# Where the weight splits and GpSimd's share run in the later stages of a two-block transformer kernel

## The chip, the cores and the metric

The program runs on one core of one Trainium2 chip. The metric is the device time of one execution in microseconds; the comparison is by the median over runs.

## The reference

The input is 256 tokens of width 1024, all in float32. The first block is a mixer, a cross attention over 256 memory rows, and a mixture of 32 experts (the best four for each token). The second block has two layers:

```python
for layer in range(2):
    h = x * (1.0 + scale) + shift
    y = mixer_ab(h, ...) if layer % 2 == 0 else mixer_c(h, ...)
    x = layer_norm(DN_ALPHA * x + gate * y, ln_g[layer, 0], ln_b[layer, 0])
    h = x * (1.0 + scale) + shift
    y = jnp.square(jax.nn.relu(h @ mlp_w1)) @ mlp_w2
    x = layer_norm(DN_ALPHA * x + gate * y, ln_g[layer, 1], ln_b[layer, 1])
```

`mixer_ab` projects h (1024 to 1224 columns), applies rope, and runs a windowed attention with sinks (8 heads) and one over the 64 best keys of an index score (8 heads). `mixer_c` has 16 heads with plain causal attention at this length. Both end in an output projection of 1024 by 1024. The MLPs go from 1024 to 4096 and back.

## The kernel before, in words

Five engines run their own programs and meet at semaphores. The file has one section for each: `block.sync` (SP, which issues the loads), `block.gpsimd`, `block.scalar` (ScalarE, ACT), `block.tensor` (TensorE, PE) and `block.vector` (VectorE, DVE).

**Weights as granules.** All weights go through a ring of 8 slots of 128 x 4096 float32 (2 MB each). One load is a granule, numbered in the order in which TensorE uses them. TensorE adds one to `granules_used` (`used`) when it has finished with one. The expert loop takes slots 0 to 5 (`E_SLOTS` is 4, 5, 2, 3, 0, 1), six granules for each of 32 experts: four of the gate and up projection, two of the down projection. The granules after the experts are, in order, ab_in (3), uq (1), ab_out (2), mlp0 (16), c_in (6), c_out (2), mlp1 (16). They land in `POST_SLOTS`, four slots in turn: 6, 7, 4, 5.

**Splits.** A product outside the experts is made in three passes over two reduced-precision parts of each operand: high by high, high by low, low by high (`three`, L1047). So each granule after the experts but uq is split before use. `split_hi` (L477, always on ScalarE) copies it to its high part; `split_lo` (L487, on VectorE or GpSimd) subtracts the high part from the raw weights to get the low part. `split_no` numbers the splits; the semaphores `w_hi` and `w_lo` count them, and each waits for the one before it. The kernel before has two pairs of high and low slots (`PAIRS`: slots 2, 3 and 0, 1), used in turn. A split can begin when TensorE is done with the split two before. A raw slot can be loaded again when both its parts are made.

**Who does what around the splits.** Each engine's order is written out by hand; a wait holds everything behind it on that engine. GpSimd makes the low parts of the first granule of each stage (ab_in 0, ab_out 0 and 1, mlp0 0, c_in 0, c_out 0 and 1, mlp1 0). It multiplies the normalised X by the norm's gain and adds its bias (`affine`, L649), for the final norm of the first block and for three layer norms; the transposed copy that feeds the matmuls has gain and bias folded in elsewhere, so this X is needed only for the next residual sum. It also ropes the window attention's queries (L424 to L427). VectorE does the other low parts, the other ropes, the masks and softmax pieces, the layer norms (`layer_norm`, L1989 to L1999), the low part of the transposed activations (`evac_lo`, L2016 and L2021), and the low part of the MLP's hidden values (L2033, L2037). ScalarE does the high parts, PSUM evacuations, exponentials and roots.

**Order at the joints.** After a layer norm, TensorE transposes X (L1412), ScalarE and VectorE write the high and low transposed chunks, and the next matmuls begin chunk by chunk (`x_chunk`). In an MLP, groups of four granules (w1, w2, w1, w2) repeat four times; ScalarE and VectorE split the granules two ahead after each pair of hidden halves. After the expert loop TensorE scatters the last expert's output (L1288), VectorE adds the sums to X (L1884) and scales it by the final norm's root (L1888). If an expert had more than 64 tokens, extra passes follow the loop, up to 16, read from a table.

The pairs and the raw slots are laid out in these lines:

```python
SLOTS = 8
R2 = 4
POST_SLOTS = [6, 7] + E_SLOTS[0:2]
PAIRS = (E_SLOTS[2:4], E_SLOTS[4:6])
```

Of the kernel before, what the change touches and what calls it, by code (L numbers as in the profile page):

```python
# [22 lines left out]
ALU = mybir.AluOpType  # L23
# [6 lines left out]
TB = S // P  # L30
D = 1024
KC = D // P
NE = 32
# [95 lines left out]
PAIRS = (E_SLOTS[2:4], E_SLOTS[4:6])  # L129
# [79 lines left out]
def build_program(nc, A, tab_d, dft_d, out_d):  # L209
    ctx = ExitStack()  # L210
    with ctx:
# [16 lines left out]
        def sb(name, shape, dt=F32):  # L228
# [8 lines left out]
                  for part, s in zip(("hi", "lo"), slots)] for i, slots in enumerate(PAIRS)]  # L237
# [53 lines left out]
        def pair(n):  # L291

            return [part[:] for part in pairs[(n - 1) % 2]]
# [171 lines left out]
        def split_hi(act, name, i, it=None):  # L465

            g = granule_no(name, i)
            n = split_no(g)
# [8 lines left out]
            act.activation(pair(n)[0][:, 0:w], slot(slot_of(g), w), ACT.Copy).then_inc(sem("w_hi"), 1)  # L477

        def split_lo(eng, name, i, it=None):
# [3 lines left out]
            hi, lo = pair(n)  # L483
# [8 lines left out]
        def _(sp):  # L492
# [67 lines left out]

            sp.wait_ge(sem("table_ready"), 1)
            n = nc.values_load(table_i[0:1, 32:33], engines=[ENG.SP], min_val=0, max_val=NX_MAX)
            with sp.If(n > 0):
                sp.wait_ge(used, MOE_END)
                with sp.Fori(0, n) as i:
                    e = nc.values_load(table_i[0:1, bass.ds(i, 1)], engines=[ENG.SP], min_val=0, max_val=NE - 1)
                    sp.wait_ge(sem("extra_used"), i + 1)
                    for j in range(PER_E):
                        sp.dma_start(slot(expert_slot(j)).rearrange("p (k n) -> p k n", k=2 if j < 4 else 4),
                                     expert_source(j, e)).then_inc(sem("extra_landed"), 16)  # L570
# [3 lines left out]
            for name, count in (("ab_in", 3), ("uq", 1), ("ab_out", 2), ("mlp0", 16), ("c_in", 6), ("c_out", 2),  # L574
                                ("mlp1", 16)):
                if name[:3] != "mlp":
                    for i in range(count):
                        o = OWNER[g]
                        if o is None:
                            sp.wait_ge(used, NPRE)  # L580
                        elif o < MOE_END:
                            sp.wait_ge(used, o + 1)
                        else:
                            sp.wait_ge(sem("w_hi"), split_no(o))
                            sp.wait_ge(sem("w_lo"), split_no(o))
                        for dst, src in granule_source(name, i, slot_of(g)):
                            sp.dma_start(dst, src).then_inc(landed[slot_of(g)], 16)
                        g += 1
                    continue
                if name == "mlp0":  # L590
                    sp.wait_ge(*done("uq", 0))
# [3 lines left out]
                with sp.Fori(0, 4) as i:  # L595
                    for j in range(R2):
                        s = slot_of(g + j)
                        n = split_no(g + j) - R2
                        sp.wait_ge(sem("w_hi"), i * R2 + n)
                        sp.wait_ge(sem("w_lo"), i * R2 + n)  # L600
# [15 lines left out]
        def _(pool):  # L616
# [24 lines left out]

            def w_lo(name, i):
                split_lo(pool, name, i)

# [1544 lines left out]
```

## Time and profile before

| | us |
|---|---|
| median of 3 runs | 2086.86 |
| all runs | 2105.39, 2086.86, 2086.72 |
| the profiled execution, whole | 2106.02 |
| its span, from first to last instruction | 2104.2 |
| busy in the span: TensorE | 1881.5 (89%) |
| VectorE | 751.7 (36%) |
| ScalarE | 538.4 (26%) |
| GpSimd | 140.7 (7%) |

The span is one profiled execution; the positions in the rows (1379.67, for example) are microseconds from its start. Busy time counts an instruction from its start to its end, whatever it waits for inside. The expert loop lies between about 350 and 1320 us, the stages that the change touches from there to the end. Line numbers such as L487 are lines of the kernel before; where a helper issues an operation, the line is the helper's. PEclk is the TensorE clock that was granted, 1.00 for full speed.

### The profile page before, as it was taken

What the parts mean: (1) busy time and instruction counts of PE and PEld (TensorE: products, weight loads), DVE (VectorE), ACT (ScalarE), POOL (GpSimd) and SP (SyncE); (2) the same over time, 40 slices, a digit from 0 to 9 for tenths busy, and PEclk for the clock granted to TensorE, in tenths of its full rate; (3) what the DMA queues carried; (4) which work ended last, traced back from release to release, by engine and by line L of the source; (5) the groups of instructions that cost most, each with busy time, mean ns of one, the idle gap of its engine ahead of it and who ended that gap; (6) DMA issues with size and microseconds to landing.
All of it is one profiled execution on the core that took longest, in us unless ns stands there. A gap on an engine that the chain in (4) does not pass through costs nothing.

```text
span 2104.2 us, 25272 instructions
## 1 busy us (share of the span) xinstructions
PE 1881.5 (89%) x10270; PEld 1155.1 (55%) x10270; DVE 751.7 (36%) x1136; ACT 538.4 (26%) x700; POOL 140.7 (7%) x49
## 2 busy tenths in 40 slices
PE   6998898999999999999999999755699979568997
PEld 6855665434444344433443344634589868357996
DVE  3323232111111111111111111477565476656555
ACT  4322341111111111111111111335334432533442
POOL 0100110000000000000000000240300030311000
PEclk9998895999999999999999999866799989888999
DMA  8488568899999999999999999440145535213450
GB/s 310 166 303 331 177 227 334 356 417 417 419 418 417 417 419 418 417 417 419 418 417 417 419 418 416 156 159 1 60 154 185 200 120 192 88 60 117 164 179 21
DMA packets 136599, 587.07 MB, mean 279 GB/s; under 512 B 6446, under 2 KB 6660, under 8 KB 102756
## 3 DMA queue, kind: packets, MB, share of 16 engines
q1 hardware_dynamic: 135108, 581.25, 70.0%
q10 hardware_dynamic: 1440, 5.11, 0.7%
q8 instruction: 36, 0.59, 0.1%
q14 instruction: 15, 0.12, 0.0%
HBM read 585.29 MB, written 1.05 MB: 279 GB/s over the span
## 4 chain that ended last, share of the span: by engine, by line
PE 62%; DMA 20%; DVE 13%; ACT 3%; issue 2%; SPq 0%; POOL 0%; ACTq 0%; DVEq 0%
PE bank L1047 29%; DMA ring<-in_w_gate_up 20%; PE bank L1255 14%; PE bank L1279 5%; PE bank L1215 3%; PE bank L1118 2%; PE bank L1288 1%; DVE sb_X L1992 1%; PE bank L1108 1%; DVE arena_r L2021 1%; DVE sb_XN L1962 1%; PE bank L1246 1%; PE bank L1381 1%; PE bank L1272 1%; DVE sb_XN L1933 1%
## 5 line engine op out<-in xcount | busy, mean ns | idle before, releaser
L1255 PE MATMUL bank<-ring,arena 128*64 128x512 f32 x2048 | 458.6, 598 | 8.0 <-DMA ring<-in_w_gate_up 8.0
L1255 PEld LDWEIGHTS bank<-ring,arena 128*64 128x64 f32 x2048 | 140.3, 137 | 321.0 <-issue 298.5
L1047 PE MATMUL bank<-w_hi,arena_r 128*128 128x512 f32 (+1 forms) x784 | 259.5, 393 | 6.5 <-DVE arena_r L2037 3.7
L1279 PE MATMUL bank<-ring,arena 128*64 128x512 f32 x1024 | 226.8, 595 | 0.0
L487 DVE TENSOR_TENSOR w_lo<-ring,w_hi 128x4096 fp32r<-128x4096 f32 (+2 forms) x37 | 161.6, 4367 | 134.0 <-ACT w_hi L477 133.8
L477 ACT ACTIVATE w_hi<-ring 128x4096 fp32r<-128x4096 f32 (+2 forms) x45 | 160.6, 3577 | 131.3 <-PE bank L1047 130.7
L1047 PEld LDWEIGHTS bank<-w_hi,arena_r 128*128 128x128 f32 x784 | 149.3, 190 | 37.2 <-DVE arena_r L2037 4.1
L487 POOL TENSOR_TENSOR w_lo<-ring,w_hi 128x4096 fp32r<-128x4096 f32 (+1 forms) x8 | 70.6, 8821 | 1366.2 <-ACT w_hi L477 1365.8
L825 ACT ACTIVATE arena<-arena,sb_tab 128x512 f32<-128x512 f32 x32 | 23.1, 722 | 530.0 <-DVE arena L1826 530.0
L1047 PE MATMUL bank<-XT_r,w_hi 128*128 128x256 f32 x512 | 147.8, 289 | 12.0 <-DVE arena_r L2021 12.0
L1800 DVE TENSOR_SCALAR arena<-sb_tab,sb_pos 128x64 f32<-128x64 f32 x66 | 13.8, 252 | 400.0 <-PE bank L1255 400.0
L1279 PEld LDWEIGHTS bank<-ring,arena 128*64 128x64 f32 x1024 | 70.7, 137 | 153.9 <-issue 153.9
L1826 DVE TENSOR_SCALAR arena<-bank 128x512 f32<-128x512 f32 x32 | 22.1, 692 | 351.5 <-PE bank L1255 351.5
L1047 PE MATMUL bank<-arena_r,w_hi 128*128 128x256 f32 x512 | 146.5, 286 | 0.0
L1047 PE MATMUL bank<-XT_r,w_lo 128*128 128x256 f32 x512 | 146.4, 286 | 0.0
L1215 PEld LDWEIGHTS bank<-arena,sb_XN 128*128 128x128 f32 x1056 | 123.7, 196 | 26.0 <-issue 26.0
L1215 PE MATMUL bank<-arena,sb_XN 128*128 128x64 f32 x1056 | 128.2, 281 | 0.0
L1047 PE MATMUL bank<-w_lo,arena_r 128*128 128x512 f32 x320 | 125.6, 392 | 0.0
L1047 PEld LDWEIGHTS bank<-XT_r,w_hi 128*128 128x128 f32 x512 | 99.7, 195 | 14.6 <-issue 14.1
L1047 PEld LDWEIGHTS bank<-arena_r,w_hi 128*128 128x128 f32 x512 | 99.9, 195 | 0.9 <-issue 0.5
L1047 PEld LDWEIGHTS bank<-XT_r,w_lo 128*128 128x128 f32 x512 | 99.9, 195 | 0.0
L462 DVE TENSOR_TENSOR half_lo<-ring,half_hi 128x2048 fp32r<-128x2048 f32 x22 | 50.4, 2292 | 85.0 <-ACT half_hi L452 84.8
(318 smaller groups left out, 2376.3 us busy)
## 6 DMA issues: line engine op xcount, KB each, us to landing
ring<-in_w_gate_up SPq DMA_DIRECT2D x128, 2048.0 KB, 23.1
ring<-in_w_down SPq DMA_DIRECT2D x64, 2048.0 KB, 22.3
ring<-in_mlp_w SPq DMA_DIRECT2D x32, 2048.0 KB, 8.2
ring<-in_ada_w SPq DMA_DIRECT2D x24, 2048.0 KB, 9.4
ring<-in_c_w_in SPq DMA_DIRECT2D x6, 2048.0 KB, 7.6
ring<-in_w_in SPq DMA_DIRECT2D x4, 2048.0 KB, 7.6
ring<-in_w_k SPq DMA_DIRECT2D x2, 2048.0 KB, 12.2
ring<-in_w_v SPq DMA_DIRECT2D x2, 2048.0 KB, 21.2
```

The lines of the kernel that those rows point to most:

```text
L462: eng.tensor_tensor(lo[:], half_raw(name, h)[1], hi[:].bitcast(F32), ALU.subtract).then_inc(sem("w_lo"), 1)
L477: act.activation(pair(n)[0][:, 0:w], slot(slot_of(g), w), ACT.Copy).then_inc(sem("w_hi"), 1)
L487: eng.tensor_tensor(lo[:, 0:w], slot(slot_of(granule_no(name, i)), w), hi[:, 0:w].bitcast(F32), ALU.subtract).then_inc(sem("w_lo"), 1)
L825: act.activation(sig, gcl, ACT.Sigmoid, bias=zero, scale=1.702).then_inc(sem("e_sig"), 1)
L1047: mm = pe.matmul(out, st[a], mv[b], start=start and a + b == 0, stop=stop and a == 1, skip_group_check=True)
L1108: mm = pe.matmul(B[7][:, c:c + 1], part[:, c * P:(c + 1) * P], quads[:, 0:1], start=True, stop=True)
L1118: mm = pe.matmul(B[6][32 * c:32 * c + 32, :], cs[:, 2 * c + r, :], w[:, 2 * c + r, :], start=(r == 0), stop=(r == 1))
L1215: mm = pe.matmul(B[3][:, k * CAP:(k + 1) * CAP], XN[:, t, k * P:(k + 1) * P], sel_tok[:, t, :], start=(t == 0), stop=(t == 1))
L1246: pe.matmul(B[m][CAP * h:CAP * h + CAP, :], selG[64 * m:64 * m + NE, :], rows[:, h * HW:(h + 1) * HW], start=True, stop=False)
L1255: mm = pe.matmul(B[m][CAP * h:CAP * h + CAP, :], xe[:, 2 * j + kl, :], w[:, kl, m * D + h * HW:m * D + (h + 1) * HW], start=False, stop=(j ...
L1279: mm = pe.matmul(B[2][CAP * h:CAP * h + CAP, :], hT[:, c, CAP * j:CAP * j + CAP], w[:, c, h * HW:(h + 1) * HW], start=False, stop=(j == 1 ...
L1826: dve.tensor_scalar(gcl, B[0][:], 7.0, None, ALU.min).then_inc(sem("e_clamp"), 1)
```

## The change

Only the work after the expert loop is touched, in six ways.

1. Slots: four granules can be split at once. The high part of a granule has one of four slots of its own (`HI_SLOTS`: 2, 3, 0, 1) and its low part is written over the raw weights. A slot is loaded again when TensorE has used the granule in it.
2. GpSimd does no low parts, no `affine` and no rope after the expert loop. VectorE does them, at other places of its order.
3. ScalarE's high parts move: ab_in 0 in the last expert (which is peeled off the loop), ab_in 1 where ab_in 0 was, c_out 0 and 1 before the values of the second attention are evacuated, mlp 0 and 1 before the gate rows, c_in 0 inside the last MLP group.
4. VectorE's order: ab_in 0 after the expert loop, ahead of the residual additions; ab_in 1 before the rope angles; ab_out 0 before the first scores; ab_out 1 and mlp0 0 and 1 before the first layer norm; the first MLP group is peeled so that the affine of the norm before stands behind it; c_in 0 in the last MLP group; c_out 0 and 1 before the second attention; mlp1 0 and 1 before the third norm.
5. SP issues ab_in 0 and 1 before it looks at the table of extra experts.
6. The extra passes use slots 4, 5, 0, 1 (`X_SLOTS`), and load the down granules after the gate and up products.

The diff, cut to its core:

```diff
-PAIRS = (E_SLOTS[2:4], E_SLOTS[4:6])
+HI_SLOTS = E_SLOTS[2:6]
+X_SLOTS = E_SLOTS[0:2] + E_SLOTS[4:6]
...
-                  for part, s in zip(("hi", "lo"), slots)] for i, slots in enumerate(PAIRS)]
+                  for part, s in zip(("hi", "lo"), slots)] for i, slots in enumerate(zip(HI_SLOTS, POST_SLOTS))]
...
-        def pair(n):
+        def pair(g):
-            return [part[:] for part in pairs[(n - 1) % 2]]
+            return [part[:] for part in pairs[(g - MOE_END) % R2]]
...
         def split_hi(act, name, i, it=None):
...
-            if n > 2 * len(SPLIT) + 2:
-                before = g - 2 - (g - 2 <= MOE_END + UQ <= g)
-                act.wait_ge(used, step + (before + 1))
+            if g < MOE_END + R2:
+                act.wait_ge(used, MOE_END - 2 if g < MOE_END + 2 else MOE_END)
             else:
-                act.wait_ge(used, MOE_END)
+                act.wait_ge(used, step + (g - R2 + 1))
...
@@ block.sync
+            def post_fill(name, i):
+                g = granule_no(name, i)
+                sp.wait_ge(used, NPRE if OWNER[g] is None else OWNER[g] + 1)
+                for dst, src in granule_source(name, i, slot_of(g)):
+                    sp.dma_start(dst, src).then_inc(landed[slot_of(g)], 16)
+
+            post_fill("ab_in", 0)
+            post_fill("ab_in", 1)
...
-                        sp.wait_ge(sem("w_hi"), i * R2 + n)
-                        sp.wait_ge(sem("w_lo"), i * R2 + n)
+                        sp.wait_ge(used, i * R2 + (g + j - R2 + 1))
...
@@ block.gpsimd
-            w_lo("ab_in", 0)
-            pool.wait_ge(sem("nfin_landed"), 16)
-            pool.wait_ge(*upto("m0", "T", 4))
-            for t in range(TB):
-                affine("fin", t)
...
-                rope_on(pool, link, out, Z[:, t, 0:512].rearrange("p (g j d) -> p j g d", j=4, g=2),
...
-            w_lo("ab_out", 0)
-            w_lo("ab_out", 1)
-            for l, after in enumerate(("mlp0", "c_in", "mlp1")):
-                w_lo(after, 0)
...
-                for t in range(TB):
-                    affine(f"ln{l}", t)
-                if after == "c_in":
-                    w_lo("c_out", 0)
-                    w_lo("c_out", 1)
...
@@ block.scalar
+                if ahead is not None:
+                    split_hi(act, *ahead)
                 act.wait_ge(*down_done)
                 act.activation(ysb, B[2][:], ACT.Copy).then_inc(sem("e_y"), 1)
...
-            with act.Fori(0, NE) as i:
+            with act.Fori(0, NE - 1) as i:
                 expert(i, (used, i * PER_E + (NPRE + PER_E)))
+            expert(NE - 1, (used, MOE_END), ("ab_in", 0))
...
-            gate_rows(0)
             load_ln(0, upto("ab", "o", 4))
             split_hi(act, "mlp0", 0)
+            split_hi(act, "mlp0", 1)
+            gate_rows(0)
             ln_root(0, 0)
-            split_hi(act, "mlp0", 1)
...
@@ block.vector
+            split_lo(dve, "ab_in", 0)
             n = nc.values_load(table_i[0:1, 32:33], engines=[ENG.DVE], min_val=0, max_val=NX_MAX)
             dve.wait_ge(sem("acc_main"), 1)
...
+            def affine(st, ts):
+                for t in ts:
+                    if st == "fin":
+                        ins = dve.tensor_tensor(X[:, t, :], X[:, t, :], nfin, ALU.mult)
+                    else:
+                        link(dve.tensor_tensor(X[:, t, :], X[:, t, :], lng, ALU.mult))
+                        ins = dve.tensor_tensor(X[:, t, :], X[:, t, :], lnb, ALU.add)
+                    ins.then_inc(sem("ln_x"), 1)
...
-            def mlp(l):
-                split_lo(dve, f"mlp{l}", 1)
+            def mlp(l, ahead):
                 for b in range(4):
                     dve.memset(B[b][:], 0.0).then_inc(sem("mlp_zero"), 1)
                 gate_diag(2 * l + 1)
-                with dve.Fori(0, 3) as it:
+                mlp_group(l, 0, False)
+                affine_ready(2 * l + 1)
+                affine(f"ln{2 * l}", range(TB))
+                with dve.Fori(1, 3) as it:
                     mlp_group(l, it, False)
-                mlp_group(l, 3, True)
+                mlp_group(l, 3, True, ahead)
...
+            dve.wait_ge(sem("z0"), 3)
+            dve.wait_ge(sem("z1"), 3)
+            rope_aq(0)
             dve.wait_ge(sem("cq_root"), 1)
...
             dve.wait_ge(sem("sink_landed"), 16)
+            split_lo(dve, "ab_out", 0)
             for u in range(2):
                 front("ab", u, tb_("window"))
...
             gate_diag(0)
+            split_lo(dve, "ab_out", 1)
+            split_lo(dve, "mlp0", 0)
+            split_lo(dve, "mlp0", 1)
             layer_norm(0, "ab_out", 1)
             evac_lo(1)
...
+            split_lo(dve, "c_out", 0)
+            split_lo(dve, "c_out", 1)
             dve.wait_ge(sem("c_rope"), 8)
             front("cc", 0, tb_("full"))
```

## Rows read from the trace of the kernel before

**Rows 1.** the page, chain of work that ended last, by engine.

```profile
PE 62%; DMA 20%; DVE 13%; ACT 3%; issue 2%; SPq 0%; POOL 0%; ACTq 0%; DVEq 0%
```

**Rows 2.** busy time by stretch: window, length, busy us (xcount) per engine, PEclk, DMA share, GB/s.

```profile
450.00:500.00 50.00, 50.00 (x254) 18.39 (x252) 6.50 (x19) 5.46 (x7) 0.00 (x0) 1.00 1.02 417
1539.60:1704.10 164.50, 164.50 (x1038) 149.27 (x1039) 82.01 (x44) 73.87 (x45) 0.48 (x1) 1.00 0.53 192
```

**Rows 3.** timeline of POOL, 1320 to 1830: start, length, line, operation, [idle before].

```profile
1323.79 7.93 POOL L487 TENSOR_TENSOR w_lo<-ring,w_hi 128x3672 fp32r<-128x3672 f32 x1 [964.99 <-ACT w_hi L477]
1336.15 4.75 POOL L649 TENSOR_TENSOR sb_X<-sb_X,arena 128x1024 f32<-128x1024 f32 x2 [4.43 <-PE bank L1412]
...
1379.54 17.98 POOL L487 TENSOR_TENSOR w_lo<-ring,w_hi 128x4096 fp32r<-128x4096 f32 x2
...
1703.62 8.95 POOL L487 TENSOR_TENSOR w_lo<-ring,w_hi 128x4096 fp32r<-128x4096 f32 x1 [176.22 <-ACT w_hi L477]
...
1805.60 18.07 POOL L487 TENSOR_TENSOR w_lo<-ring,w_hi 128x4096 fp32r<-128x4096 f32 x2 [71.86 <-ACT w_hi L477]
```

**Rows 4.** timeline of DVE, 1320 to 1415, same columns.

```profile
1322.20 2.48 DVE L1884 TENSOR_TENSOR sb_X<-bank,sb_X 128x512 f32<-128x512 f32 x4 [10.90 <-PE bank L1288]
...
1328.15 4.79 DVE L1888 TENSOR_SCALAR sb_X<-sb_X,sb_stat 128x1024 f32<-128x1024 f32 x2
...
1336.78 4.26 DVE L2021 TENSOR_SCALAR arena_r<-sb_XN,sb_mod 128x256 fp32r<-128x256 f32 x2
...
1341.86 0.62 DVE L2021 TENSOR_SCALAR arena_r<-sb_XN,sb_mod 128x256 fp32r<-128x256 f32 x2
...
1379.67 8.85 DVE L426 TENSOR_TENSOR sb_XN<-arena,sb_ropeS 128x64 f32<-128x64 f32 x1
...
1404.64 0.69 DVE L424 TENSOR_TENSOR arena<-bank,sb_ropeC 128x512 f32<-128x512 f32 x1
...
1413.88 0.56 DVE L1933 SCALAR_TENSOR_TENSOR sb_XN<-bank,sb_tab 128x384 f32<-128x384 f32 x1 [4.84 <-PE bank L1366]
```

**Rows 5.** timeline of DVE, 1704 to 1830.

```profile
1705.46 8.19 DVE L1992 SCALAR_TENSOR_TENSOR sb_X<-sb_X,sb_XN 128x1024 f32<-128x1024 f32 x1
...
1717.82 1.23 DVE L1992 SCALAR_TENSOR_TENSOR sb_X<-sb_X,sb_XN 128x1024 f32<-128x1024 f32 x1
...
1724.79 4.24 DVE L2021 TENSOR_SCALAR arena_r<-sb_XN,sb_mod 128x256 fp32r<-128x256 f32 x2
...
1736.79 4.42 DVE L487 TENSOR_TENSOR w_lo<-ring,w_hi 128x4096 fp32r<-128x4096 f32 x1
...
1803.11 1.02 DVE L1933 SCALAR_TENSOR_TENSOR sb_XN<-bank,sb_tab 128x384 f32<-128x384 f32 x2 [12.74 <-PE bank L1366]
...
1807.39 7.08 DVE L1942 TENSOR_SCALAR sb_att<-sb_att 128x4 f32<-128x4 f32 x1
...
1814.58 9.64 DVE L1962 TENSOR_TENSOR sb_XN<-sb_XN,sb_att 128x256 f32<-128x256 f32 x2
```

**Rows 6.** timeline of ACT at the end of the expert loop.

```profile
1320.45 3.26 ACT L477 ACTIVATE w_hi<-ring 128x3672 fp32r<-128x3672 f32 x1 [0.56 <-issue]
```

**Rows 7.** DMA issues of 1280 to 1290.85: queue, count, KB, us to landing.

```profile
ring<-in_ab_w_in SPq DMA_DIRECT2D x1, 1836.0 KB, 27.1
```

**Rows 8.** timeline of PE, the query projection of the second block.

```profile
1378.98 9.68 PE L1519 MATMUL bank<-ring,XT 128*128 128x512 f32 x16 [0.97 <-DVE XT L2068]
```

**Rows 9.** timeline of DVE, end of the first output projection.

```profile
1498.34 1.29 DVE L1989 TENSOR_TENSOR sb_XN<-bank,sb_XN 128x512 f32<-128x512 f32 x2 [17.84 <-PE bank L1047]
```

**Rows 10.** timeline of PE, start of the first MLP.

```profile
1522.86 0.55 PE L1047 MATMUL bank<-XT_r,w_hi 128*128 128x256 f32 x1 [5.14 <-DVE arena_r L2021]
...
1528.87 0.35 PE L1047 MATMUL bank<-XT_r,w_hi 128*128 128x256 f32 x1 [0.22 <-DVE arena_r L2021]
```

**Rows 11.** waits of PE in the first MLP: us in total, times, longest.

```profile
PE bank L1047 <- DVE arena_r L2037: 1.9, 1, 1.9
```

**Rows 12.** the page, DMA issues: count, KB each, median us to landing.

```profile
ring<-in_mlp_w SPq DMA_DIRECT2D x32, 2048.0 KB, 8.2
```

More of the change, by code:

```diff
@@ L577, in _ @@
                     for i in range(count):
[L578 to L587, printed above, removed]
+                        if (name, i) not in POST[0:2]:
+                            post_fill(name, i)
                         g += 1
                     continue
-                if name == "mlp0":
-                    sp.wait_ge(*done("uq", 0))
                 l = int(name[3])
@@ L820, in _, with expert @@
             ada(4)
-            def expert(i, down_done):
+            def expert(i, down_done, ahead=None):
                 act.wait_ge(sem("e_clamp"), 2 * i + 1)
@@ L872, in evac_hi, with mlp_group @@
                                        bias=g0(k)).then_inc(sem("xt_a"), 1)
-            def mlp_group(l, it, last):
+            def mlp_group(l, it, last, ahead=None):
                 n = f"mlp{l}"
@@ L891, in mlp_group @@
                         split_hi(act, n, 2 * p + 3, it)
+                    if p == 0 and ahead is not None:
+                        split_hi(act, *ahead)
             def exps(st, u):
@@ L926, in _ @@
             evac_hi(0)
-            split_hi(act, "ab_in", 1)
+            split_hi(act, "ab_in", 2)
             act.wait_ge(sem("rope_ang"), 1)
@@ L988, in _ @@
                 split_hi(act, "c_in", i)
+            split_hi(act, "c_out", 0)
+            split_hi(act, "c_out", 1)
             act.wait_ge(*done("c_in", 5))
@@ L1452, in mlp_group @@
                     pe.wait_ge(sem("w_lo"), it * R2 + split_no(g))
-                    w = chunks(pair(split_no(g)), KC)
+                    w = chunks(pair(g), KC)
                     for b in range(2):
@@ L1464, in mlp_group @@
                     pe.wait_ge(sem("w_lo"), it * R2 + split_no(g))
-                    w = chunks(pair(split_no(g)), 4)
+                    w = chunks(pair(g), 4)
                     if p == 0:
@@ L2023, in evac_lo, with mlp_group @@
                 dve.wait_ge(*upto(f"m{a}", "xt_v", KC))
-            def mlp_group(l, it, last):
+            def mlp_group(l, it, last, ahead=None):
                 n = f"mlp{l}"
@@ L2041, in mlp_group @@
                         split_lo(dve, n, 2 * p + 3, it)
-            def mlp(l):
-                split_lo(dve, f"mlp{l}", 1)
+                    if p == 0 and ahead is not None:
+                        split_lo(dve, *ahead)
+            def mlp(l, ahead):
                 for b in range(4):
@@ L2143, in _ @@
                 split_lo(dve, "c_in", i)
+            affine_ready(2)
+            affine("ln1", range(TB))
             tmps = XNf.rearrange("p (i n) -> p i n", i=4)
```

108 lines of the change are left out of this document (47 added, 61 removed).

## The prediction

> **What bounds the kernel now.** I read the chain of waits first, then busy time by stretch, then the timelines of GpSimd and VectorE side by side. In the chain TensorE holds 62%, DMA 20% and VectorE 13%, GpSimd 0% [rows 1]. By stretch the expert loop (one window of it stands) moves 417 GB/s with the queues full, and the two MLPs (one row stands) keep TensorE busy for all of their 164.5 us at clock 1.00 [rows 2]. Nothing that the change edits can shorten either: it loads the same bytes and issues the same matmuls. So I look at the joints between them, where VectorE sets the pace.
>
> There the timelines show one pattern. While GpSimd runs a tensor_tensor, a VectorE instruction that normally takes a microsecond or less ends only when GpSimd's ends. A 128x64 product takes 8.85 us (1379.67 to 1388.52) beside the first of two GpSimd splits that begin at 1379.54 and take 9 us each; its neighbour after it is held as long by the second [rows 3, 4]. L1992 takes 8.19 us beside a split, 1.23 us without one; L2021 4.26 or 4.24 us a pair beside GpSimd's affine, 0.62 us without; L1942, on 4 columns, 7.08 us and L1962 9.64 us beside the two c_out splits [rows 3 to 5]. GpSimd's 0% in the chain hides this: the wait is booked as VectorE's work.
>
> **The change part by part.** *Stalls that go.* GpSimd does nothing after the expert loop any more. Excess over the undisturbed length: L1888 starts at 1328.15 and is held until the first split ends at 1331.72, at most 3.6 us, taken as 3.2 (by L1992's 1.23 for the same width it would be 4.79 - 2.46 = 2.3 at least); L2021 in the final norm 3.6; the two rope instructions 8.6 and 8.5 (one stands); L1992 in three layer norms about 7.0 each (the one row's 8.19 - 1.23; the others a little less, take 6.5); L2021, two pairs in each of three norms, 3.6 + 3.5; L1942 6.9, L1962 8.6 [rows 4, 5]. Together about 80 us of stall. What of it is on the path differs by place.
>
> *Work that comes.* VectorE takes seven full splits of 4.42 us and a shorter one, 35 us; fourteen 1024-wide products, priced by L1992's 1.23, 17 us; two ropes of 512 columns, at most four instructions of 0.69 each, 5 us [rows 4, 5]. In all 57 us. The cover of each follows.
>
> *End of the expert loop: a loss.* ScalarE now makes the high part of ab_in 0 before the last expert's output copy. That load was issued at 1290.82 and landed 27.1 us later, at 1317.9 [rows 7]. Copy 3.26 us to 1321.2; the output copy, which ended 0.56 us before 1320.45, now ends at about 1321.8, 1.9 us late [rows 6]. VectorE's low part of it runs from 1321.2 to about 1325.6, in front of the residual additions that began at 1322.20 [rows 4]. Loss 3 us, from 0 (landing earlier) to 4. The extra-expert path was not entered: the additions follow directly on the last scatter, so its reordering is worth nothing.
>
> *Final norm and ab_in.* 3.2 us of L1888 is all on the path. Of L2021's 3.6 I take 2.5, as TensorE already begins on the first chunk. The other two splits of ab_in on VectorE lie beside its matmuls. Gain 5.7.
>
> *Projections and rope.* The second query projection takes 9.68 us from 1378.98 [rows 8], and the last rope, which began at 1404.64 [rows 4], needs it plus the transposes behind it, for which I allow 2 us: with the start 1 us earlier, 1389.7. Gain 15.0, less than the 17.1 of stall, because TensorE is next. Two ropes of 2 to 2.8 us go before it, in the waits for ScalarE's root and for the transposes. The ab_out 0 split stands before the first scores; the idle there was 4.84 us [rows 4] against 4.42. Cost 0, up to 4.4 if that cover is gone.
>
> *Three layer norms.* Splits of ab_out 1, mlp 0 and 1 (13.3 us, and 1.2 for the gate's 1024-wide product) lie in VectorE's idle 17.84 us before the norm [rows 9]: nothing. L1992's stall goes in full, 6.5, 7.0, 6.6; then TensorE's own end is level with the second half of the norm. Before each MLP, 24 matmuls took from 1522.86 to 1528.87 for want of chunks [rows 10]; starting 3.6 us earlier and fed without a stop they take between 3.8 us (the MLP's mean spacing, 164.5 us over 1038 [rows 2], times 24) and 6.0. The first matmul took 0.55 us against 0.35 later, so they are slow at first: I take 4.4, which makes the gain 5.2, from 3.6 to 5.8. The split, which ended the 1.9 us wait for the first hidden low part [rows 11], is done earlier: 1.9 more. So 13.6 for each MLP entry. Before c_in each chunk feeds 12 matmuls of 512 columns, so the second L2021 stall is hidden anyway: 1.4 from the first and 1.0 from the second split, 9.4 with L1992. Affines (5 us each) go behind the first MLP group and into c_in, where VectorE is half idle [rows 2].
>
> *Attention of the second layer.* 6.9 + 8.6 = 15.5 us, all on the path [rows 5]. The two c_out splits (8.9 us) go ahead of the scores, where VectorE idled 12.74 us [rows 5].
>
> *Four granules.* A slot's low part overwrites its raw weights, so a refill waits for TensorE, not for the split. The MLPs had no matmul gap to win [rows 2]: 0, and no loss while a load lands in 8.2 us [rows 12]. SP's refills all stand in the same order as before.
>
> **Sum:** -3 + 5.7 + 15 + 13.6 + 9.4 + 15.5 + 13.6 = 69.8 us. The profiled execution took 2106.02 us, so 2036. It was a long one: of the runs shown two are at 2086.8 and one at 2105.4, so against the median I get 2086.86 - 69.8 = 2017. I take 2018.
>
> **A rule against it.** By the rows GpSimd holds VectorE for one instruction at a time and nearly to its own end. The Trainium skill ("Perfetto Trace Analysis", Optimizing Scalar/DVE Operations) says that because the two engines share a port, moving operations between them might not help. Here the rows agree on the sharing; whether the move helps hangs on cover, and the rival below prices it. The skill ("SBUF — State Buffer", Who interferes with whom) names instructions with two SBUF inputs among those that contend; L1989, with one PSUM input, kept its 1.29 us beside a split, which fits.
>
> **Rivals.** *The time moves with the work (8%).* If none of the moved 57 us were covered, the gain would be about 80 less the 7 of stall already hidden, less 57 and 3: 13 to 20 us, or 2067 to 2074. For it: the covers before the first scores and the c_out splits are tight, 0.4 and 3.8 us. Against: half of VectorE's time in the MLPs is idle. A partial form (10%), those two covers and a late affine lost, costs 5 to 20 us: 2023 to 2038.
>
> *The median falls on the upper level (13%).* The profile before and one run were 19 us long for a cause that I don't see; with two such of three, 2036.
>
> *The clock stays up (8%).* TensorE now idles less after each projection; if the granted clock did not fall, slow matmuls at three entries give 2 to 3 us each: 2010.
>
> *The stalls are not GpSimd's (3%).* VectorE would keep them, and the covered work costs little: 2085 to 2095. Against it: the ends coincide at every place.
>
> *Slower (4%): refills tied to TensorE.* A slot's round becomes landing + 3.6 (high) + 4.4 (low) + 10.3 (matmuls; 164.5 us over 16 granules), and four slots give 41 us. It decides from a landing of 22.8 us on; the load at the loop's end took 27.1 [rows 7], but behind a full queue, and an MLP has two loads out at most. To turn the gain into a loss of 1% the 32 granules must each lose (70 + 21)/32 = 2.9 us, a landing of 34 us: 2108.
>
> **Numbers.** My forecast holds 54%: 2005 to 2031, from the bounds of the loss at the loop's end, of the MLP entries, of the ab_out 0 cover and 10% of the stalls. The range goes to 2004 for the clock case and 2040 for the upper level and the partial form; outside are about 2 in 10. A measurement of this kernel can tell about 1% (21 us) from no change. Faster by more: 54 + 13 + 10 + 8, and 1 of the uncovered case's 8, 86%. Within: the other 7 and the 3 of the stalls that stay, 10%. Slower: 4%.
>
> **What would show it.** L2021 at 0.3 us each, L1992 at 1.23 and L1962 at about 0.5 everywhere, GpSimd empty after 1320: each stall term. The first scores some 15 us closer to the end of ab_in. The first MLP matmul without a wait for splits, and MLPs still 164 us long; a wait for a load in them would be the slower rival. A VectorE split that ends after its first scores or after TensorE's last output-projection matmul would be lost cover. If L1992 stays near 8 us with GpSimd empty, the reading is wrong altogether.

## The result and the profile after

The changed kernel takes 2031.16 us in the median of four runs (2029.46 to 2035.42); the kernel before, over four runs, 2095.78 us (2086.72 to 2105.39). The ratio is 0.969, with a 95% interval of 0.963 to 0.976. The forecast was 2018 us with a range of 2004 to 2040, and faster. The profiled execution took 2029.46 us (span 2027.4); that of before took 2106.02.

The changed kernel's page, first engines, then the chain of what ended last:

```profile
PE 1870.2 (92%) x10270; PEld 1148.0 (57%) x10270; DVE 725.2 (36%) x1166; ACT 536.1 (26%) x699; POOL 29.2 (1%) x19
...
PE 68%; DMA 20%; DVE 7%; ACT 3%; issue 1%; POOL 0%; SPq 0%; DVEq 0%; ACTq 0%
...
ring<-in_mlp_w SPq DMA_DIRECT2D x32, 2048.0 KB, 8.3
```

The change shows in two numbers. VectorE's share of the chain fell from 13% to 7% [rows 1]. And its busy time fell from 751.7 to 725.2 us, although it took on work that the prediction put at 57 us. Both kernels' mlp loads land as fast [rows 12].

VectorE's timeline in the changed kernel (start, length, line, operation, [idle before]), through the stretches of [rows 4, 5]:

```profile
1317.73 3.98 DVE L486 TENSOR_TENSOR w_lo<-ring,w_hi 128x3672 fp32r<-128x3672 f32 x1 [9.94 <-ACT w_hi L476]
1321.63 2.48 DVE L1837 TENSOR_TENSOR sb_X<-bank,sb_X 128x512 f32<-128x512 f32 x4
...
1326.64 1.42 DVE L1841 TENSOR_SCALAR sb_X<-sb_X,sb_stat 128x1024 f32<-128x1024 f32 x2
...
1331.90 0.62 DVE L1992 TENSOR_SCALAR arena_r<-sb_XN,sb_mod 128x256 fp32r<-128x256 f32 x2
...
1384.97 4.42 DVE L486 TENSOR_TENSOR w_lo<-ring,w_hi 128x4096 fp32r<-128x4096 f32 x1
1389.67 0.56 DVE L1886 SCALAR_TENSOR_TENSOR sb_XN<-bank,sb_tab 128x384 f32<-128x384 f32 x1 [0.28 <-PE bank L1318]
...
1474.05 1.29 DVE L1942 TENSOR_TENSOR sb_XN<-bank,sb_XN 128x512 f32<-128x512 f32 x2 [4.44 <-PE bank L998]
1475.37 1.23 DVE L1945 SCALAR_TENSOR_TENSOR sb_X<-sb_X,sb_XN 128x1024 f32<-128x1024 f32 x1
...
1685.34 13.49 DVE L486 TENSOR_TENSOR w_lo<-ring,w_hi 128x4096 fp32r<-128x4096 f32 x3
...
1734.46 8.95 DVE L486 TENSOR_TENSOR w_lo<-ring,w_hi 128x4096 fp32r<-128x4096 f32 x2
1755.33 1.02 DVE L1886 SCALAR_TENSOR_TENSOR sb_XN<-bank,sb_tab 128x384 f32<-128x384 f32 x2 [11.92 <-PE bank L1318]
...
1757.43 0.17 DVE L1895 TENSOR_SCALAR sb_att<-sb_att 128x4 f32<-128x4 f32 x1
```

Each stalled instruction is back at its short length: the scaling of the final norm 1.42 us for two where it took 4.79, the evacuation pair (now L1992) 0.62 where it took 4.26, the layer norm's 1024-wide instruction (now L1945) 1.23 where it took 7.7 to 8.2, the 128x4 one (now L1895) 0.17 where it took 7.08. The new splits stand where VectorE waited: the one before the first scores leaves 0.28 us of idle, the two before the second attention leave 11.92.

**A ruler of joints.** A time of the whole run hides where a gain lies. So I took the start of ten VectorE instructions that both kernels have, and the distance of each from the one before it. All times are microseconds of the two profiled executions; their starts are rows of VectorE's timelines.

| joint, up to | before | after | gained |
|---|---|---|---|
| last expert's clamp starts, at | 1306.90 | 1303.39 | |
| residual additions | +15.30 | +18.24 | -2.9 |
| scaling of the final norm | +5.95 | +5.01 | 0.9 |
| end of ab_in | +41.53 | +34.58 | 7.0 |
| first scores | +44.20 | +28.45 | 15.7 |
| first layer norm | +84.46 | +84.38 | 0.1 |
| second layer norm | +205.80 | +192.73 | 13.1 |
| first scores, second attention | +98.97 | +88.55 | 10.4 |
| third layer norm | +74.38 | +60.48 | 13.9 |
| last norm | +207.56 | +192.50 | 15.1 |
| end of the span | +19.15 | +19.09 | 0.1 |
| from the clamp to the end | 797.3 | 724.0 | 73.3 |

This ruler repeats. From the clamp to the end, two profiled runs of before gave 797.3 and 797.5 us, and two of the changed kernel 724.0 and 724.0, although their spans differ by up to 19.4 us: that difference arises ahead of the clamp, where nothing was changed. Below I call this distance the tail, and judge every experiment by it. Single joints repeat less well. Against the first profiled run of before, the second has 0.9 us less up to the end of ab_in, 1.2 less up to the first layer norm, 1.6 more up to the second and 0.8 more up to the third; in the tail these cancel. So a difference of 1 to 2 us at one joint, in one trace, may be chance.

### The profile page after: what moved, and what is told of

Read it like the earlier page. It is cut to its first block, busy times and chain, and to the rows that moved or that the text cites. A ratio compares the mean times of both kernels' runs of the same rounds, so it can differ in the third digit from the quotient of the medians.

```text
span 2027.4 us, 25205 instructions
## 1 busy us (share of the span) xinstructions
PE 1870.2 (92%) x10270; PEld 1148.0 (57%) x10270; DVE 725.2 (36%) x1166; ACT 536.1 (26%) x699; POOL 29.2 (1%) x19
## 4 chain that ended last, share of the span: by engine, by line
PE 68%; DMA 20%; DVE 7%; ACT 3%; issue 1%; POOL 0%; SPq 0%; DVEq 0%; ACTq 0%
PE bank L998 32%; DMA ring<-in_w_gate_up 18%; PE bank L1206 15%; PE bank L1230 6%; PE bank L1166 3%; PE bank L1069 2%; PE bank L1239 2%; PE bank L1059 1%; DMA ring<-in_ab_w_in 1%; PE bank L1197 1%; PE bank L1333 1%; PE bank L1223 1%; DVE sb_XN L1886 1%; DVE sb_XN L1915 1%; DVE sb_rt L1947 1%
## 5 line engine op out<-in xcount | busy, mean ns | idle before, releaser
L486 DVE TENSOR_TENSOR w_lo<-ring,w_hi 128x4096 fp32r<-128x4096 f32 (+2 forms) x45 | 196.5, 4367 | 53.4 <-ACT w_hi L476 51.0
L774 ACT ACTIVATE arena<-arena,sb_tab 128x512 f32<-128x512 f32 x32 | 23.1, 722 | 531.0 <-DVE arena L1778 531.0
L783 ACT ACTIVATE arena<-bank 128x512 f32<-128x512 f32 x32 | 19.1, 596 | 230.5 <-PE bank L1230 230.5
## 6 DMA issues: line engine op xcount, KB each, us to landing
ring<-in_w_gate_up SPq DMA_DIRECT2D x128, 2048.0 KB, 23.1
```

Of the source, the lines that this page charges most:

```text
L486: eng.tensor_tensor(lo[:, 0:w], slot(slot_of(granule_no(name, i)), w), hi[:, 0:w].bitcast(F32), ALU.subtract).then_inc(sem("w_lo"), 1)
L774: act.activation(sig, gcl, ACT.Sigmoid, bias=zero, scale=1.702).then_inc(sem("e_sig"), 1)
```

## The experiments

**The changed kernel again**, unchanged, as the reference on the chip of the next three.

> The changed kernel once more, as the reference for the three kernels beside it. Expected 2030 us, as in its four runs so far (2029.5 to 2035.4). The kernel before had two levels in its runs, 2087 and 2105. If these come from how GpSimd and VectorE meet, the changed kernel has only one level; if they come from the chip or the expert loop, it shows a second one some 18 us off as well.

It took 2031.56 us (2029.83 to 2035.23), ratio to before 0.967 (0.962 to 0.971). Ratios are to the runs of before on the same chip: their median was 2103.24 us for this and the next three kernels, and 2097.22 for the three on the next chip. The tail is 724.0 again. The level of the faster runs of before, which the last section tells of, did not appear in its four.

**Before, GpSimd's work cut short.**

```diff
-            w = width(name, i)
+            w = cut or width(name, i)
...
-                split_lo(pool, name, i)
+                split_lo(pool, name, i, cut=None if name == "ab_in" else 16)
...
-                    ins = pool.tensor_tensor(X[:, t, :], X[:, t, :], row, op)
+                    ins = pool.tensor_tensor(X[:, t, 0:16], X[:, t, 0:16], row[:, 0:16], op)
```

> The kernel before, with all orders and slots as they were, but GpSimd's low parts (except that of ab_in 0) and affines cut to 16 columns, so part of the values is left out; nothing is added to VectorE. Theory (VectorE is held by GpSimd's instructions): the stalls go without any move of work: 2.5 us in the final norm, 15 at the rope, 12 at each MLP entry with its norm, 8 at c_in, 11 in the second attention (ScalarE's two c_out high parts stay in front of the exponentials there), some 60 us in all, span 2044. Rival (the long VectorE instructions have another cause, for example the loads or ScalarE): L1992 stays at 7 to 8 us and the span at 2095 to 2104.

Two more places belong to this version. Where a low part is cut, TensorE reads the high part in its place, or at the MLPs what the slot held, so it does the same number of matmuls on other values; and VectorE's split of ab_in 1 is 4096 columns wide instead of 3672. GpSimd's ropes stay whole.

Measured: 2030.58 us (2027.52 to 2036.82), ratio 0.966 (0.961 to 0.971), tail 730.8. With nothing moved, and the old order of everything else, cutting GpSimd's work short gives 66.5 of the 73.3 us. That is more than I expected of it and leaves 6.8 for all the rest. By joint, what it lacks against the changed kernel is 4.8 in the second attention, 2.8 up to the end of ab_in (the stall of the final norm stands, 4.78 us beside the split that was left), 1.7 up to the first scores, and it is 2.9 ahead at the end of the expert loop. The rival by which the stalls were VectorE's own falls here. GpSimd and VectorE, the kernel before with GpSimd cut short:

```profile
1321.09 7.92 POOL L487 TENSOR_TENSOR w_lo<-ring,w_hi 128x3672 fp32r<-128x3672 f32 x1 [965.00 <-ACT w_hi L477]
1333.44 0.40 POOL L649 TENSOR_TENSOR sb_X<-sb_X,arena 128x16 f32<-128x16 f32 x2 [4.42 <-PE bank L1413]
```

```profile
1325.44 4.78 DVE L1889 TENSOR_SCALAR sb_X<-sb_X,sb_stat 128x1024 f32<-128x1024 f32 x2
...
1334.08 0.62 DVE L2022 TENSOR_SCALAR arena_r<-sb_XN,sb_mod 128x256 fp32r<-128x256 f32 x2
```

The first instruction still meets a full GpSimd split and is still held to its end (1325.44 + 4.78 is 1330.22; the split ends at 1329.01, and one of the two instructions runs after it). The second meets a 16-column product and takes 0.62.

**After, the moved work cut short.**

```diff
-                        ins = dve.tensor_tensor(X[:, t, :], X[:, t, :], nfin, ALU.mult)
+                        ins = dve.tensor_tensor(X[:, t, 0:16], X[:, t, 0:16], nfin[:, 0:16], ALU.mult)
...
-            split_lo(dve, "ab_out", 0)
+            split_lo(dve, "ab_out", 0, cut=16)
```

> The changed kernel, with the moved low parts of ab_in 0, ab_out 0 and 1, c_in 0, c_out 0 and 1 and all fourteen affine products cut to 16 columns (their values are left out; the first pass of the MLPs' first granule stays whole). This takes about 43 of the 57 us of moved work off VectorE. Theory (the moved work is covered): only the split at the end of the expert loop and half a microsecond at the first scores were on the path, 2 to 4 us faster than the changed kernel. Rival (the time moves with the work): 20 to 40 us faster.

Measured: 2025.53 us (2021.32 to 2032.09), ratio 0.964 (0.959 to 0.970), tail 724.25 against 724.0. I expected 2 to 4 us and got none. VectorE's busy time fell by 39.5 us (725.4 to 685.9), and that part of the work that came to it costs nothing; the first splits of the MLPs and the ropes stayed whole, and no run takes them away. The median is 6 us under that of the changed kernel beside it, but not by the tail: the profiled run is 10.9 us ahead of that kernel's at the clamp already. The one on the path, ab_in 0's low part ahead of the additions, brings 1.1 us when cut, and the final norm's scaling comes 1.1 later after them. The joint there shows why it is so little:

```profile
1312.59 0.17 DVE L487 TENSOR_TENSOR w_lo<-ring,w_hi 128x16 fp32r<-128x16 f32 x1 [9.94 <-ACT w_hi L477]
1315.35 2.48 DVE L1838 TENSOR_TENSOR sb_X<-bank,sb_X 128x512 f32<-128x512 f32 x4 [2.59 <-PE bank L1240]
```

Without the split VectorE waits 2.59 us for TensorE, which had itself waited 2.49 us for ScalarE's late output copy.

**After, with two split granules at once instead of four.**

```diff
-HI_SLOTS = E_SLOTS[2:6]
+PAIRS = (E_SLOTS[2:4], E_SLOTS[4:6])
...
-            split_lo(dve, "mlp0", 1)
...
             def mlp(l, ahead):
+                split_lo(dve, f"mlp{l}", 1)
...
-            mlp(0, ("c_in", 0))
+            mlp(0, None)
+            split_lo(dve, "c_in", 0)
```

The same is done for mlp1 and for ScalarE's high parts; the rest stays on VectorE as in the change.

> The changed kernel with two pairs of high and low slots as before, and so with the second MLP granule split after the norm and the first c_in granule split just ahead of the norm that follows the MLP; refills still wait for TensorE. Theory (four slots are worth what they let stand elsewhere): 4 us at the norm after the first MLP, 2 at each MLP entry, 1 at c_in, 1 at the other norms, 8 to 10 us slower than the changed kernel. Rival (the slots are worth nothing, all of the gain is GpSimd's leaving): 0 to 2 us.

Measured: 2053.14 us (2052.55 to 2055.91), ratio 0.977 (0.973 to 0.982), tail 747.1, 23.1 longer. The expectation missed by more than half. By joint: 8.1 up to the second layer norm, 10.8 up to the second attention, 4.5 up to the last norm. The c_in stage shows how, VectorE and then ScalarE of this kernel:

```profile
1671.78 4.42 DVE L487 TENSOR_TENSOR w_lo<-ring,w_hi 128x4096 fp32r<-128x4096 f32 x1 [2.76 <-ACT w_hi L477]
1676.12 1.28 DVE L1944 TENSOR_TENSOR sb_XN<-bank,sb_XN 128x512 f32<-128x512 f32 x2
...
1694.77 4.43 DVE L487 TENSOR_TENSOR w_lo<-ring,w_hi 128x4096 fp32r<-128x4096 f32 x1
1707.68 4.43 DVE L487 TENSOR_TENSOR w_lo<-ring,w_hi 128x4096 fp32r<-128x4096 f32 x1 [8.49 <-ACT w_hi L477]
```

```profile
1704.02 3.63 ACT L477 ACTIVATE w_hi<-ring 128x4096 fp32r<-128x4096 f32 x1 [12.43 <-PE bank L1000]
1714.90 3.63 ACT L477 ACTIVATE w_hi<-ring 128x4096 fp32r<-128x4096 f32 x1 [7.25 <-PE bank L1000]
```

With two pairs ScalarE may not make the third high part before TensorE has used the first (12.43 us of wait, then 7.25 for each), so VectorE's splits come one by one between TensorE's granules, and the first of them stands in front of the layer norm, which begins 4.3 us late. With four, three low parts are made in one go at 1685.34. So my "four granules: 0" was wrong as a term: four are what lets VectorE do the splits in its idle time. The 23.1 us are for two pairs together with the orders that they force. Whether four would shorten anything with GpSimd's work left where it was has no run.

**Before again**, one run, on the chip of the following three.

> The kernel before once more, for one more trace. If it falls on its lower level (2087 us, 18 us under the first trace), the two traces of one kernel show where the levels part: at a joint where GpSimd and VectorE meet (theory), with one or two of the long VectorE instructions short, or in the expert loop or the clock (rival).

It took 2086.62 us (span 2084.8), 19.4 less than the first profiled run, and the tail is 797.5 against 797.3. So in total these two runs differ only ahead of the last expert, and not where GpSimd and VectorE meet behind it, as the theory had it.

**After, with c_out's splits put back.**

```diff
-            split_hi(act, "c_out", 0)
-            split_hi(act, "c_out", 1)
             act.wait_ge(*done("c_in", 5))
...
+            split_hi(act, "c_out", 0)
+            split_hi(act, "c_out", 1)
             exps("cc", 0)
...
+            split_lo(pool, "c_out", 0)
+            split_lo(pool, "c_out", 1)
```

> The changed kernel, with the two c_out low parts back on GpSimd and their high parts on ScalarE back in front of the exponentials. Theory: the stalls of the second attention come back (L1942 of the kernel before 7 us, L1962 some 9 us), 14 to 16 us slower than the changed kernel, and nothing elsewhere. Rival (VectorE had room there): 0 to 3 us slower, since the two splits leave VectorE.

Measured: 2041.04 us (2035.32 to 2047.19), ratio 0.972 (0.967 to 0.976), tail 740.3, 16.3 longer, of which 15.6 lie between the first scores and the third layer norm. GpSimd, then VectorE of this kernel:

```profile
1758.64 18.08 POOL L486 TENSOR_TENSOR w_lo<-ring,w_hi 128x4096 fp32r<-128x4096 f32 x2 [1402.46 <-ACT w_hi L476]
```

```profile
1760.43 7.08 DVE L1897 TENSOR_SCALAR sb_att<-sb_att 128x4 f32<-128x4 f32 x1
...
1767.62 9.64 DVE L1917 TENSOR_TENSOR sb_XN<-sb_XN,sb_att 128x256 f32<-128x256 f32 x2
```

The two stalls return to the hundredth: 7.08 and 9.64, as in [rows 5].

**After, with the affines back on GpSimd.**

```diff
+                for t in range(TB):
+                    if a == 0:
+                        ins = pool.tensor_tensor(X[:, t, :], X[:, t, :], nfin, ALU.mult)
...
-                affine_ready(2 * l + 1)
-                affine(f"ln{2 * l}", range(TB))
```

> The changed kernel, with the gain and bias products of X back on GpSimd at the transposes. Theory: the low parts of the transposed chunks are held again, 4 us a pair twice in each norm: 2.5 us at ab_in, 5 at each MLP entry, 1.5 at c_in, 12 to 15 us slower, though VectorE has 17 us less to do. Rival (the load on VectorE is what counts): 0 to 5 us faster.

Measured: 2037.48 us (2026.45 to 2051.55), ratio 0.972 (0.967 to 0.977), tail 742.4, 18.4 longer. Four places lose: 2.8 up to the end of ab_in, 5.7, 3.5 and 6.2 after the three norms. GpSimd, then VectorE at the first norm:

```profile
1474.69 2.34 POOL L649 TENSOR_TENSOR sb_X<-sb_X,arena 128x1024 f32<-128x1024 f32 x1 [154.14 <-PE bank L1380]
1477.11 2.34 POOL L652 TENSOR_TENSOR sb_X<-sb_X,arena 128x1024 f32<-128x1024 f32 x1
1479.41 2.43 POOL L649 TENSOR_TENSOR sb_X<-sb_X,arena 128x1024 f32<-128x1024 f32 x1
1481.92 2.37 POOL L652 TENSOR_TENSOR sb_X<-sb_X,arena 128x1024 f32<-128x1024 f32 x1
```

```profile
1475.39 4.21 DVE L2008 TENSOR_SCALAR arena_r<-sb_XN,sb_mod 128x256 fp32r<-128x256 f32 x2
...
1480.42 4.02 DVE L2008 TENSOR_SCALAR arena_r<-sb_XN,sb_mod 128x256 fp32r<-128x256 f32 x2
```

9.5 us of GpSimd hold four short VectorE instructions for 8.2 us where they need 1.2, and 5.7 of the 7.0 reach TensorE. I had taken 12 to 15 us for the four places together. The largest part of the miss is c_in, 3.5 us where I had 1.5. TensorE waits 2.72 us for the first low chunk where the changed kernel waits 1.28 for a high one; and VectorE's next c_in split stands behind both stalled pairs, so TensorE waits once more:

```profile
1690.30 0.50 PE L1014 MATMUL bank<-w_hi,XT_r 128*128 128x512 f32 x1 [1.67 <-DVE w_lo L486]
```

**After, with ab_in 0's split behind the last expert's output.**

```diff
-            with act.Fori(0, NE - 1) as i:
+            with act.Fori(0, NE) as i:
                 expert(i, (used, i * PER_E + (NPRE + PER_E)))
-            expert(NE - 1, (used, MOE_END), ("ab_in", 0))
...
+            split_lo(dve, "ab_in", 0)
             dve.wait_ge(*upto("fin", "root", 1))
```

ScalarE's high part of ab_in 0 then stands ahead of the final norm's squares, that of ab_in 1 behind them.

> The changed kernel with the split of ab_in 0 moved behind the last expert's output copy on ScalarE and behind the residual additions on VectorE, and the high part of ab_in 1 behind the final norm's squares. Theory: the additions start 2.9 us earlier against the loop's end, the low part then delays the root's reciprocal by about 0.8, so 1 to 2 us faster than the changed kernel, at the limit of what can be timed but plain in the trace. Rival (the low part of ab_in 0 becomes late for TensorE): 1 to 3 us slower.

Measured: 2028.03 us (2010.57 to 2032.2), ratio 0.966 (0.962 to 0.969), tail 722.0. VectorE there:

```profile
1301.91 2.48 DVE L1836 TENSOR_TENSOR sb_X<-bank,sb_X 128x512 f32<-128x512 f32 x4 [10.91 <-PE bank L1239]
1304.32 3.97 DVE L486 TENSOR_TENSOR w_lo<-ring,w_hi 128x3672 fp32r<-128x3672 f32 x1
1308.21 0.16 DVE L1839 RECIPROCAL sb_stat<-sb_stat 128x2 f32<-128x2 f32 x1
```

The additions follow the clamp by 15.30 us, as before the change, and the split runs in the wait for ScalarE's statistics. It gives back the 2.9 us of the loss at the loop's end and takes 1.5 at the norm. By the tail, one trace of each, it is 2.0 us better than the changed kernel and the shortest of the versions that leave nothing out; the medians (2028.03 and 2031.16) can't tell the two apart.

**After, c_out's high parts late, with no GpSimd work.** The 66.5 us left one question: the second attention lacked 4.8 us there, although no stall was left.

```diff
-            split_hi(act, "c_out", 0)
-            split_hi(act, "c_out", 1)
             act.wait_ge(*done("c_in", 5))
...
+            split_hi(act, "c_out", 0)
+            split_hi(act, "c_out", 1)
             exps("cc", 0)
...
+            split_lo(pool, "c_out", 0, cut=16)
+            split_lo(pool, "c_out", 1, cut=16)
```

> Changed kernel with one order put back: ScalarE makes the two high parts of c_out again right before the exponentials of the second attention (3.6 us each), and no longer in the last projection. To take GpSimd out of it, the two low parts are 16 columns wide (TensorE reads the high part in their place). Theory A: the 15.5 us that I put down to VectorE's stalls hid a second wait of about the same length: exponentials behind 7.3 us of ScalarE's splits. Then first scores to the third layer norm take 4 to 6 us longer than the changed kernel's 60.5, as in the kernel before with GpSimd's work cut short (65.3). Theory B: that 4.8 us there came from something else in the old order; here within 1 us of 60.5.

Measured in one run: 2015.98 us, tail 725.0; first scores to third layer norm 64.3 against 60.5, 3.8 longer, a little under the 4 to 6 of theory A. VectorE of this kernel:

```profile
1742.66 0.17 DVE L1898 TENSOR_SCALAR sb_att<-sb_att 128x4 f32<-128x4 f32 x1
1747.50 0.18 DVE L1915 RECIPROCAL sb_att<-sb_att 128x4 f32<-128x4 f32 x1 [4.67 <-ACT sb_XN L857]
```

The exponentials wait behind 7.23 us of high parts on ScalarE, and VectorE then waits 4.67 us for them. The kernel before with GpSimd cut short has the same wait there, 4.66 us. In the trace of before the stall lay over this wait and hid it.

**After, c_out's full low parts on GpSimd, early.** It asks whether the engine or the place was at fault.

```diff
-            split_lo(dve, "c_out", 0)
-            split_lo(dve, "c_out", 1)
...
+            split_lo(pool, "c_out", 0)
+            split_lo(pool, "c_out", 1)
```

> Changed kernel, its high parts of c_out made where it makes them, but the two full low parts on GpSimd (9 us each) as soon as these are there. They should run from about 1730 to 1749, while VectorE still has c_in splits and ropes until 1743 and then idles 11.9 us before the scores at 1755. Theory A: GpSimd's work costs only what it overlaps of VectorE's, and the place, not the engine, was the fault: first scores to third layer norm stay at 60.5 within 1 us, the c_in stage loses at most 4 us, and the whole stays within 4 us of the changed kernel (back with both of e6's places it lost 16). Theory B: any full split on GpSimd costs its length on the path: 9 to 18 us.

Measured in one run: 2029.38 us, tail 723.7 against 724.0. GpSimd, then VectorE:

```profile
1726.95 9.03 POOL L486 TENSOR_TENSOR w_lo<-ring,w_hi 128x4096 fp32r<-128x4096 f32 x1 [1371.33 <-ACT w_hi L476]
1737.90 9.51 POOL L486 TENSOR_TENSOR w_lo<-ring,w_hi 128x4096 fp32r<-128x4096 f32 x1 [1.92 <-ACT w_hi L476]
```

```profile
1727.96 8.58 DVE L428 TENSOR_TENSOR arena<-arena,sb_XN 128x512 f32<-128x512 f32 x1
...
1739.82 8.14 DVE L428 TENSOR_TENSOR arena<-arena,sb_XN 128x512 f32<-128x512 f32 x1
...
1755.87 1.02 DVE L1888 SCALAR_TENSOR_TENSOR sb_XN<-bank,sb_tab 128x384 f32<-128x384 f32 x2 [5.92 <-PE bank L1320]
```

The stalls are as long as ever, 8.58 and 8.14 where the instruction takes 0.69, but they fall where VectorE had 11.92 us to spare; the scores begin 0.5 us later after the norm and the third norm 0.3 us earlier. The same two splits, on the same engine, cost 15.6 us together with the late high parts and nothing here.

## Why the prediction was right, and where it was not

**The sum.** I had 69.8 us; the tail gave 73.3. Term by term, predicted and measured: the end of the loop -3 and -2.0 net (the additions 2.9 late, 0.9 regained before the norm); final norm and ab_in 5.7 and 7.0; projections and rope 15.0 and 15.7; first norm and MLP 13.6 and 13.1; second norm and c_in 9.4 and 10.4; second attention 15.5 and 13.9; third norm and MLP 13.6 and 15.1. No other joint moved by over 0.1 us. Measured against the second profiled run of before, the final norm with ab_in gives 6.0, the first norm and MLP 14.7, the second attention 14.7, and the first layer norm moves 1.1 us the other way, so none of the differences of 1.6 us or less from my terms can be read as an error of a term by itself.

**GpSimd's hold** carried the sum and was right: 66.5 of the 73.3 us come with its work cut short and nothing else moved, and each of two groups put back brought its stalls back. That VectorE's stall is off the path when it falls into idle time is shown as well. It bears on the rule cited against the change from the Trainium skill ("Perfetto Trace Analysis", Optimizing Scalar/DVE Operations), that moving work between the two engines might not help. The traces agree that the two get in each other's way (7.08 us beside a split for what takes 0.17 alone), yet here the move took 73.3 us off, since the work could be put where VectorE idled.

**The cover** held: 0.28 us was left before the first scores, and the 39.5 us of moved work that were cut short gained nothing. The rival "the time moves with the work" is refuted by the 73.3 us; the partial one too, since the covers that it doubts are among what was cut.

**The MLP entries.** TensorE's timeline at the first one, changed kernel:

```profile
1488.61 0.55 PE L998 MATMUL bank<-XT_r,w_hi 128*128 128x256 f32 x1 [1.55 <-DVE arena_r L1992]
1488.96 0.41 PE L998 MATMUL bank<-arena_r,w_hi 128*128 128x256 f32 x1
...
1493.61 0.28 PE L998 MATMUL bank<-XT_r,w_lo 128*128 128x256 f32 x1
```

The first matmul had 1.55 us of idle before it where it had 5.14 [rows 10], and the first ones still take 0.55 and 0.41 us in place of 0.28. The granted clock was 0.50 from 1484 to 1493.5 us, so it did fall, and the rival by which it stays up is out. TensorE's waits from 1460 to 1830 list neither a load nor a low part of weights, and the MLP's window is full of matmuls, as in [rows 2]: refills tied to TensorE cost nothing, and the slower rival falls. The window:

```profile
1501.30:1665.80 164.50, 164.50 (x1044) 149.45 (x1043) 91.69 (x49) 78.19 (x48) 0.00 (x0) 1.00 0.54 192
```

**The second attention, the step that was mis-sized.** I took L1942's 6.9 and L1962's 8.6 us as all on the path and cost ScalarE's high parts, which the change moves too, at nothing. The stall is one of two waits that lay over each other. Without GpSimd 9.1 us go (74.4 to 65.3 in before with GpSimd cut short), and the remaining 4.8 need ScalarE's earlier high parts, of which 3.8 were shown by themselves in the changed kernel. Together 13.9. Of the 1.6 us that are missing, 1.2 lie in a stretch of transposes and value products shortly before the output projection: 4.63 us in the changed kernel where the first trace of before has 3.43, at a granted clock of 0.63 against 1.00. The change need not be its cause, for the second trace of before has it too; against that one the term is 14.7, and 9.9 go without GpSimd. The output projection behind it takes the same time in all three. Windows of the changed kernel, of before, and of before's second trace:

```profile
1790.00:1794.63 4.63, 4.26 (x20) 2.80 (x20) 1.90 (x4) 2.11 (x7) 0.00 (x0) 0.63 0.00 0
```

```profile
1852.84:1856.27 3.43, 2.83 (x20) 2.06 (x21) 1.90 (x4) 2.01 (x7) 0.00 (x0) 1.00 0.00 0
```

```profile
1832.27:1836.90 4.63, 4.34 (x20) 2.96 (x21) 1.90 (x4) 2.11 (x7) 0.00 (x0) 0.63 0.00 0
```

The change did both, so the sum held; had it moved GpSimd's work alone, this term would have been about 6 us too large.

**Four granules.** I priced them at 0, apart from 1.9 at each MLP entry and 1.0 at c_in. Undone, with the orders that hang on them, the changed kernel loses 23.1 of its 73.3 us. The "cover" that I counted for the splits ahead of the norms exists only because four can be split at once: I took for a property of VectorE's timeline what is a property of the buffers. With GpSimd's splits nearly free, two pairs lost at most the 6.8 us that the rest of the change brings; with full splits on VectorE they lose 23.1. The step had the right value only in the presence of the others.

**The median.** 2017 was the lower level of before (2086.86) less 69.8; the profiled run's own sum gave 2036. The four runs of the changed kernel, 2029.46 to 2035.42, all lay on the upper level, which is the rival that I gave 13%. So the miss of 13 us is the level and not the change, which gave 3.5 us more than my sum: from 2106.02 the measured 73.3 leads to 2032.7. That the time lies in my range is owed to the room above 2031 that I had left for this rival and the partial one, not to the forecast's own bounds, 2005 to 2031. SP's earlier issue of ab_in and the reordered extra passes have no run of their own.

## What to carry to other kernels

When a short VectorE instruction ends just when a GpSimd tensor_tensor does, book its excess to GpSimd, and ask what VectorE would do in that time: an overlap with VectorE's idle time was free here, even at 9 us a split, and one with its critical joints was not (5.7 us before the first MLP for 9.5 us of GpSimd). Before work is moved onto a half-idle engine, look for the buffer that lets it run ahead: without room for more than two split granules the same move lost nearly a third of its gain. And where an instruction is stalled, look for a second wait beneath the stall; compare kernels from a joint behind the last unchanged stage, since what lies ahead of it may vary by more than one of these edits is worth.

## What the runs showed of the hardware

**A level that is set early.** Before's runs spread from 2086.72 to 2108.79 us; its two profiled spans are 2104.2 and 2084.8. Nearly all of the difference, 19.2 us, is there when the first expert's clamp starts, at 384.87 us in the first and 365.68 in the second, and the tail is equal. The version with the later split of ab_in 0 spreads in the same way, 2010.57 to 2032.2, so the levels don't come from how GpSimd and VectorE meet behind the experts. Of the 19.2 us, 10.9 are there at VectorE's cast (L1844) at 351.54 us in the first run and 340.60 in the second, and 16.8 at its first product of the experts (L1822), at 364.54 and 347.75. The columns of these windows are length, busy us per engine, granted clock, DMA share and GB/s. Before, first profiled run:

```profile
350.00:360.00 10.00, 9.26 (x48) 6.21 (x49) 0.51 (x3) 1.88 (x2) 0.81 (x4) 0.50 0.97 353
360.00:370.00 10.00, 9.13 (x38) 5.51 (x39) 2.63 (x5) 0.00 (x0) 0.00 (x0) 0.50 0.25 100
```

The second is 11 to 17 us ahead there, so about the same work lies 10 us earlier:

```profile
340.00:350.00 10.00, 8.39 (x76) 5.76 (x77) 2.53 (x7) 1.88 (x2) 0.81 (x4) 1.00 1.01 412
350.00:360.00 10.00, 10.00 (x48) 3.29 (x46) 2.17 (x9) 0.00 (x0) 0.00 (x0) 1.00 1.03 418
```

In the longer run TensorE stands on its lower level (1.2 GHz) here, and the loads fall to 100 GB/s; in the shorter it has the upper level (2.4 GHz), and they stay at 412 and 418. The shorter run has a stretch on the lower level too, from 320 to 330 us, but a shorter one. That the clock makes the difference was not tried, and what decides it stays open.

**A hold is not shorter for a smaller instruction.** Beside a full GpSimd split, 128x4, 128x64, 128x512 and 128x1024 on VectorE all took 7.1 to 8.9 us ([rows 4, 5], and L428 above); the length is that of what is left of GpSimd's instruction, to within the instruction's own. Not every VectorE instruction is held. Those seen with an operand in PSUM were not: the layer norm's first addition took 1.29 us beside a split [rows 9], and 1.29 alone. Nor were two reductions from SBUF inside the first c_out split of before: 0.42 and 0.68 us at 1806.34 and 1806.68, and 0.42 and 0.68 in the changed kernel, where GpSimd does nothing.
